# A root on ScalarE behind three norms, smaller first scalings, and fewer constant products

## Time and profile before

| what | value |
|---|---|
| median of three runs | 754.87 us (750.48 to 756.18) |
| the profiled execution | 753.83 us, span 752.0 us |
| mean granted clock of PE | 0.989 of full speed |
| busy share of PE, DVE, ACT, POOL | 94%, 71%, 50%, 12% |
| table loads on ACT | 5: at 0.74 (Silu), 125.40 (Exp), 244.27 (Silu), 491.11 (Exp), 572.80 us (Silu) |
| PE's wait before the first transposes of norms 1, 2, 3 | 1.14, 0.67, 0.67 us |
| first matmul of the unit behind norms 1, 2, 3 | 231.06, 436.54, 559.60 us |

### The profile page before, as it was taken

How to read it: one execution, slowest core, us unless ns; L and a number is a source line. 1 busy time by engine, 2 the same in 40 slices (tenths; PEclk the granted TensorE clock), 3 DMA queues, 4 the chain that set the end, 5 groups by cost and what they waited for, 6 DMA issues and landing times. The chain is left out here.

```text
span 752.0 us, 10760 instructions
## 1 busy us (share of the span) xinstructions
PE 708.6 (94%) x3897; PEld 581.5 (77%) x3897; DVE 531.7 (71%) x1001; ACT 374.3 (50%) x696; POOL 89.1 (12%) x175
## 2 busy tenths in 40 slices
PE   4799999889899999999999999888999999999997
PEld 2577769678787888878878887777888888878886
DVE  2356687899588889887786578977578765555544
ACT  2355555567246544444423379675455544444431
POOL 7021211000020111221111100600001000000000
PEclk9999999999899999999999999999899999999999
DMA  8997994122075999998788382601338856655521
GB/s 288 354 370 223 362 357 167 29 83 87 1 252 144 366 323 330 343 327 293 273 318 308 99 216 63 224 1 57 122 103 266 264 170 188 194 178 167 183 98 56
DMA packets 93743, 155.09 MB, mean 206 GB/s; under 512 B 5980, under 2 KB 68065, under 8 KB 93697
## 3 DMA queue, kind: packets, MB, share of 16 engines
q1 hardware_dynamic: 80768, 111.24, 44.8%
q0 software_dynamic: 12928, 43.24, 17.0%
HBM read 151.32 MB, written 1.05 MB: 203 GB/s over the span
## 5 line engine op out<-in xcount | busy, mean ns | idle before, releaser
L753 ACT ACTIVATE w_hi<-raw 128x1024 fp32r<-128x1024 f32 (+3 forms) x198 | 201.5, 1025 | 262.7 <-PE lin L1777 238.5
L1098 DVE TENSOR_TENSOR w_lo<-raw,w_hi 128x1024 fp32r<-128x1024 f32 (+3 forms) x198 | 233.3, 1186 | 119.5 <-ACT w_hi L753 119.1
L1775 PE MATMUL lin<-w_hi,st_hi 128*128 128x512 f32 (+2 forms) x568 | 227.8, 401 | 2.4 <-DVE w_lo L1098 2.0
L1777 PE MATMUL lin<-w_hi,st_lo 128*128 128x512 f32 (+2 forms) x568 | 220.0, 387 | 0.0
L1776 PE MATMUL lin<-w_lo,st_hi 128*128 128x512 f32 (+2 forms) x568 | 219.6, 387 | 0.0
L1775 PEld LDWEIGHTS lin<-w_hi,st_hi 128*128 128x128 f32 x568 | 108.2, 190 | 28.4 <-issue 5.2
L1777 PEld LDWEIGHTS lin<-w_hi,st_lo 128*128 128x128 f32 x568 | 107.9, 190 | 21.5
L1776 PEld LDWEIGHTS lin<-w_lo,st_hi 128*128 128x128 f32 x568 | 108.2, 190 | 19.4 <-issue 0.7
L609 POOL DMA_DIRECT2D ada_ring<-in_ada_w_dram x80 | 42.6, 532 | 390.2 <-DVE acc L1182 305.5
L1182 DVE SCALAR_TENSOR_TENSOR acc<-ada_ring,cond_b,acc 128x1024 f32<-128x1024 f32 x64 | 81.9, 1279 | 2.9 <-DMA ada_ring<-in_ada_w_dram 2.7
L1775 PE MATMUL lin<-w_hi,hid_hi 128*128 128x512 f32 x176 | 70.1, 398 | 0.0
(11 more groups left out here) (259 smaller groups left out, 859.2 us busy)
## 6 DMA issues: line engine op xcount, KB each, us to landing
raw<-in_ffn_w_in_dram SPq DMA_DIRECT2D x88, 512.0 KB, 5.2
ada_ring<-in_ada_w_dram POOLq DMA_DIRECT2D x80, 512.0 KB, 6.0
raw<-in_ffn_w_out_dram SPq DMA_DIRECT2D x22, 1024.0 KB, 4.9
raw<-in_nsa_w_in_dram SPq DMA_DIRECT2D x10, 1024.0 KB, 12.7
ada_first<-in_ada_w_dram SPq DMA_DIRECT2D x8, 1024.0 KB, 13.1
raw<-in_nsa_cmp_w_dram SPq DMA_DIRECT2D x4, 1024.0 KB, 10.7
raw<-in_nsa_w_out_dram SPq DMA_DIRECT2D x4, 1024.0 KB, 9.1
raw<-in_mla_w_out_dram SPq DMA_DIRECT2D x4, 1024.0 KB, 5.3
```

Source lines behind the costliest of these rows:

```text
L753: nc.scalar.activation(part_of(w_hi, s), raw_part(s), ACT.Copy).then_inc(hi_ready, 1)
L1098: nc.vector.tensor_tensor(part_of(w_lo, s), raw_part(s), part_of(w_hi, s).bitcast(F32), ALU.subtract).then_inc(lo_ready, 1)
L1775: nc.tensor.matmul(bank, a_h, w_h, start=first, stop=False)
L1777: return nc.tensor.matmul(bank, a_l, w_h, start=False, stop=last)
```

## The change

For norms 1 to 3 the reciprocal root is made in another way. ACT runs a one-column Sqrt ahead of the squares. When both squares of the first half of the columns are there, DVE computes half of the mean plus epsilon (`half_mean`, one instruction between its two updates). Behind each square of the second half ACT takes the root of sum/1024 plus that half (`mean_root`), for one token tile. DVE computes the mean itself beside it, then the reciprocal of the roots and one Newton step of three instructions on it. The scaling goes in pieces of 256, 256 and 512 columns, `xn_ready` counts three per norm, and PE waits for the second piece ahead of its third batch. The constant products ahead of the transposes go from 21 at each norm to 16, 15 and 15.

```diff
-IDLE_FIRST, IDLE_SECOND = (21, 21, 21), 5
+IDLE_FIRST, IDLE_SECOND = (16, 15, 15), 5
@@ before_norm, on ACT
+                def mean_root(t):
+                    act.wait_ge(squares, 4 * k + 2 + t + 1)
+                    nc.scalar.activation(stat[:, 2, 2 + t:3 + t], stat[:, 0, 2 + t:3 + t], ACT.Sqrt,
+                                         scale=1.0 / D, bias=stat[:, 2, t:t + 1]).then_inc(rooted, 1)
+
+                nc.scalar.activation(table_root[:], ones[:, 0:1], ACT.Sqrt)
                 if not column_halves:
                     high_to(s + 2)
                 squares_of_x(k, 0)
                 squares_of_x(k, 1, [0])
+                act.wait_ge(half_ready, k)
+                mean_root(0)
                 high_to(s + 2)
                 squares_of_x(k, 1, [1])
+                mean_root(1)
                 high_to(s + 4)
@@ on DVE
+            def half_mean(k):
+                dve.wait_ge(squares, 4 * k + 2)
+                nc.vector.tensor_scalar(stat[:, 2, 0:T], stat[:, 0, 0:T], 1.0 / D, EPS, ALU.mult,
+                                        ALU.add).then_inc(half_ready, 1)
+
+            def normalise_rooted(k):
+                counts["squares"] += 2 * T
+                dve.wait_ge(squares, counts["squares"])
+                v, y, a = (stat[:, j, 0:T] for j in (1, 3, 4))
+                nc.vector.scalar_tensor_tensor(v, stat[:, 0, T:2 * T], 1.0 / D, stat[:, 2, 0:T], ALU.mult, ALU.add)
+                dve.wait_ge(rooted, 2 * k)
+                link(nc.vector.reciprocal(y, stat[:, 2, T:2 * T]))
+                link(nc.vector.scalar_tensor_tensor(a, y, -0.5, y, ALU.mult, ALU.mult))
+                link(nc.vector.tensor_tensor(a, a, v, ALU.mult))
+                link(nc.vector.scalar_tensor_tensor(y, a, 1.5, y, ALU.add, ALU.mult))
+                for c0, w in ((0, 256), (256, 256), (512, 512)):
+                    for t in range(T):
+                        ins = nc.vector.tensor_scalar(scratch[:, t * D + c0:t * D + c0 + w], x[:, t, c0:c0 + w],
+                                                      stat[:, 3, t:t + 1], None, ALU.mult)
+                    ins.then_inc(xn_ready, 1)
@@ at norm 1 (norms 2 and 3 alike)
             update_x(U_OUT0, 0, 0, (slot_used, OUT0 + 4))
+            half_mean(1)
             update_x(U_OUT0 + 1, 0, 1, (slot_used, OUT0 + 8), 1)
-            normalise_x()
+            normalise_rooted(1)
@@ x_batch, on PE
-                if k0 in (0, KD // 2):
+                if k0 in (0, KD // 2) or (k0 == 2 and batch0 != T_H0):
                     next_tokens()
```

More of the change, by code:

```diff
@@ L242, in trunk @@
         table_exp = sb("table_exp", [P, 1], F32)
+        table_root = sb("table_root", [P, 1], F32)
         nmax = sb("nmax", [P, 4, 2], F32)
@@ L353, in trunk @@
         squares = sem("squares")
+        half_ready = sem("half_ready")
+        rooted = sem("rooted")
         xn_ready = sem("xn_ready")
@@ L1594, in _ @@
             update_x(U_DOWN0, 1, 0, (part_done, 2))
+            half_mean(2)
             update_x(U_DOWN0 + 1, 1, 1, (slot_used, DOWN0 + FK), 3)
             low_to(DOWN0 + FK + 1)
-            normalise_x()
+            normalise_rooted(2)
             modulated(IN1)
@@ L1754, in _ @@
             low_to(OUT1 + 10)
+            half_mean(3)
             update_x(U_OUT1 + 1, 0, 1, (slot_used, OUT1 + 8), 4)
-            normalise_x()
+            normalise_rooted(3)
             modulated(UP1)
```

## The result

The changed kernel takes 757.07 us in the median (753.93 to 758.92, 17 runs), the kernel before 753.82 (17 runs beside them): a ratio of 1.0046, 95% interval 1.0032 to 1.0059, or 3.5 us more (2.4 to 4.4). The forecast was 0.8 us more.

The account below looks back on a forecast made before the run. TensorE, nearly full, bounds the kernel, so time won or lost at a norm reaches the end. Norm 1 +2.9, norm 2 -0.95, Sin +0.2, norm 3 -1.35 gave +0.8 us: median 755.7 us, range 750.0 to 759.5.

Parts of the forecast that it names:

- Root on ScalarE: Last square to first scaling at each norm: about 1.08 us instead of 2.18, a gain of 1.10 us.
- Half of the mean: DVE waits for ACT's second square between updates: 0.95 us later at norm 1, covered on DVE at norms 2 and 3.
- The table: Square root's table load ahead of each norm: ACT loses 1.5 us, which moves DVE, POOL and DMA at norm 1.
- Rival 2: Other DMA traffic covers the load ahead of norm 1: whole -2.0 us, 752.9, or 751.9 with the half-mean wait covered; chance 0.20.
- The Sin: One more table load before the Sin; ACT ends at 465.4 instead of 464.1, costing 0.2 us.
- What a load costs: Table load on ACT: takes 1.28 us, next instruction starts 0.01 us after it; 1.29 us with surroundings.
- rival 4: Table loads on ACT: each costs more than its own time; size not in the text given; chance 0.02.
- Pieces: Scaling in 256-column pieces: first tokens 0.26 us sooner, DVE held 0.27 us longer; the 0.27 counts at norm 1.
- Norms 2 and 3: First st_lo after the last square comes 0.95 us sooner at norm 2 and 1.35 us sooner at norm 3.
- Clock at norm 1: PE gap of 2.4 us before norm 1's transposes halves the granted clock, costing 0.5 to 2.1 us, taken as 1.3.
- Rival 3: Clock falls at norms 2 and 3 too, 2.4 us at each; +6.4 us in all, 761.3; chance 0.08.
- the sum itself: Whole kernel: norm 1 +2.9, norm 2 -0.95, the Sin +0.2, norm 3 -1.35; in all +0.8 us.

Follow-up runs that it names:

- the pair of kernels: Changed kernel without its tile, load later and half mean earlier: ratio 0.9964; the same with four 512-column pieces at norms 1 and 2: 751.14 us, ratio 0.9967.
- late_load: Changed kernel without its new tile, norm 1's one-column root and table load moved behind the weight copies: 752.32 us, ratio 0.9992 against the kernel before.

## Why the prediction was right or wrong

The direction of the sum and the time within 1% were right; the size, +0.8 against +3.5 us, was not. The forecast took about 1% for what a measurement can tell; the interval here is 1.0 us to either side, 0.13%. Point by point:

- **Root on ScalarE.** Right. From the end of the last square (229.72) to the first scaling (230.86) it is 1.14 us; forecast 1.08. The root with its pointer bias takes 0.29 us, not the 0.20 that I took from a record without one. DVE's four instructions took 0.79 instead of 0.83.
- **Half of the mean.** Right: a stall at norm 1 alone. 0.95 forecast, 0.9 won by taking it away.
- **The table.** Right: 1.5 forecast, 1.6 in the mean of the profiles. Rival 2, a landing that covers the load, falls. On PE, the stretch from the end of the attention to the constants is 30.2 us in the mean of the six profiles with the early load and 28.9 in the other eight: 1.3, forecast 1.0. The Sin costs DVE a wait of 0.27 us; forecast 0.2.
- **What a load costs.** Each of the nine loads of the changed kernel takes 1.28 us. Behind each of the eight after the first, the next instruction starts 0.01 or 0.02 us after the load's end, so rival 4, by which a load costs ACT more than its own time, falls.
- **Pieces.** 0.27 us forecast at norm 1, 0.2 shown by the pair of kernels; nothing at norm 2, which was inside the -0.95.
- **Norms 2 and 3.** Right. From the constants to the first matmul -0.92 and -1.38 us; forecast -0.95 and -1.35.
- **Clock at norm 1.** It fell, with a gap of 2.21 us (2.4 forecast). The sum's 1.3 us for it (0.5 ahead of the first matmul, 0.8 behind) rests on my estimate of how long the low clock would last, and no run shows the term as such. The runs show a clock that is low for 3.4 us in both profiles of the changed kernel and for 6.8 in both without its tile, at a cost of 0.35 us ahead of the first matmul and 0 to 2.0 behind it. The rule behind the forecast, that a gap longer than all those that passed costs the clock, doesn't hold up: 2.19 to 2.25 us fell four times and 2.24 held once, behind another order of ACT, and the gaps of 1.29 and 1.74 us, which the forecast read as costing the clock from one profile, did so in ten and eight of fourteen. That it fell at norm 1, as forecast, is in part luck. Rival 3 falls: no low clock at norms 2 and 3.
- **The step that failed is the sum itself.** It had a term for each instruction of the change and none for its one new tile, which I had read as a place to write a result that nobody needs. The tile stands ahead of the stationary operands of both down products, and with it there each product takes 1.7% longer (0.233 for 0.229 us): +1.0 us twice. With 0.8 + 2.0 = 2.8 us the forecast would lie inside the interval of 2.4 to 4.4. The other terms are less sure as a sum than one by one: the stretches around the three norms give 2.04 - 0.92 - 1.38 = -0.3 us, and the low clock behind norm 1 adds 0 to 2.0, so that +0.8 is borne out only within the 0.1 to 2.6 of the kernel without the tile.

Open: which starts of `hid_hi` are slow; what besides the gap decides the clock at norm 1; why the low clock lasts 3.4 us in one execution and 6.8 in another.

## What to carry to other kernels

A change of declarations is a change of the kernel: compare the stages that the edit doesn't touch too, and if their matmul spacing differs, try the kernel before with the new tiles alone. Put a table load where the engine waits anyway, and a wait for another engine behind an instruction that can run meanwhile; here these two moves turned +1.3 us into -2.7. When an unchanged stretch varies by 4 us between executions, measure from an event just ahead of the edit.

## What the runs showed of the hardware

- The 128x512 matmuls of the down product start every 0.233 us in the five profiles with `table_root` declared ahead of their stationary operands (two of the changed kernel, and the kernel before with an unused tile of one, two or eight columns), and every 0.229 in the nine others, with no such tile or with it behind `hid_lo`.
- A one-column ACTIVATE with a pointer bias takes 0.29 us, one without 0.20.
- Behind nearly equal gaps of PE (2.19 to 2.25 us, four profiles of the change's own order and one of late_load) the clock fell four times and held once. Around the end of an unchanged gap of 1.29 us it fell in ten profiles of fourteen.
- Where it fell at these two places it was low for 3.4 or for 6.8 us. In the latent attention these cost 1.1 to 1.8 and 2.2 to 3.1 us.
